# An expert's gate/up product in two halves with two signals, in place of one product with one signal

## The reference

```python
def hier_moe(x, rg_w, rg_b, re_w, re_b, w_gu, w_down):
    ...                                   # router: 2 of 32 experts for each of 512 tokens
    padded = (counts + MOE_BLOCK - 1) // MOE_BLOCK * MOE_BLOCK
    ...                                   # tokens sorted by expert, in blocks that belong to one expert each
    def expert_block(args):
        xb, e = args
        hg, hu = jnp.split(xb @ w_gu[e], 2, axis=-1)    # w_gu[e]: 1024 x 1024, gate and up
        return (jax.nn.silu(hg) * hu) @ w_down[e]       # w_down[e]: 512 x 1024
    y = lax.map(expert_block, (x_buf, block_e)).reshape(n_rows, D)
    y = y * gate_buf[:, None].astype(y.dtype)
    out = jax.ops.segment_sum(y, tok_buf, num_segments=n_tok + 1)[:n_tok]
```

## Time and profile before

| | |
|---|---|
| runs | 3419.12, 3424.94, 3429.10 us |
| profiled execution: time, span | 3429.10, 3427.3 us |
| TensorE busy, matmul / weight load | 87% / 63% of the span |
| VectorE, ScalarE, GpSimd busy | 38%, 26%, 8% |
| L1950 (gate/up), matmul | 414.7 us busy, 134.6 us idle before it |
| L1935 (gather), matmul | 204.6 us busy |
| L1960 (down), matmul | 195.3 us busy, 23.0 us idle before it |
| weight queue (q1) | 601.98 MB, 48.0% of 16 engines |

### The profile page before, as it was taken

One profiled execution on the slowest core, in us unless ns is written; L12 is line 12 of the kernel. 1 busy time (PEld: TensorE's weight loads), 2 busy tenths in 40 slices (PEclk: granted clock), 3 DMA queues, 4 the chain that ended last, 5 costly groups with the idle time before them and its releaser, 6 DMA issues. The chain is left out here.

```text
span 3427.3 us, 66223 instructions
## 1 busy us (share of the span) xinstructions
PE 2981.8 (87%) x27679; PEld 2155.2 (63%) x27679; DVE 1306.6 (38%) x2324; ACT 878.6 (26%) x1554; POOL 285.6 (8%) x361
## 2 busy tenths in 40 slices
PE   7998889999898799999987899865799898899766
PEld 5765567878773678877856576532467766566432
DVE  3254434332454443322163322211587544322112
ACT  3244432221335222122262200001443333100001
POOL 1013310000302000000000000000110530000000
PEclk9999999999999899999998899987799999999997
DMA  7423223324325233242211999998222214999996
GB/s 202 103 80 142 99 48 100 92 74 116 86 62 205 61 109 98 78 118 75 73 68 58 426 388 425 426 427 357 70 59 76 57 35 157 426 425 425 427 426 274
DMA packets 375756, 638.62 MB, mean 186 GB/s; under 512 B 90437, under 2 KB 327666, under 8 KB 339450
## 3 DMA queue, kind: packets, MB, share of 16 engines
q1 hardware_dynamic: 350025, 601.98, 48.0%
q10 hardware_dynamic: 21264, 23.88, 2.0%
q0 software_dynamic: 4256, 9.68, 0.8%
HBM read 611.06 MB, written 24.38 MB: 185 GB/s over the span
## 5 line engine op out<-in xcount | busy, mean ns | idle before, releaser
L1950 PE MATMUL moe_ps<-moe_ring,moe_scratch 128*32 128x256 f32 x6464 | 414.7, 409 | 134.6 <-DMA moe_ring<-in_moe_w_gu 117.1
L1950 PEld LDWEIGHTS moe_ps<-moe_ring,moe_scratch 128*32 128x32 f32 x6464 | 250.2, 117 | 288.8 <-issue 141.1
L2138 DVE TENSOR_TENSOR moe_scratch<-moe_scratch,moe_ps 128x128 f32<-128x128 f32 x102 | 39.5, 387 | 653.9 <-ACT moe_scratch L2008 653.9
L212 PE MATMUL ffn_in_ps<-ffn_xhi,ffn_in_whi 128*128 128x512 f32 x704 | 280.8, 399 | 9.0 <-DVE ffn_xlo L408 9.0
L213 PE MATMUL ffn_in_ps<-ffn_xlo,ffn_in_whi 128*128 128x512 f32 x704 | 280.5, 398 | 0.0
L214 PE MATMUL ffn_in_ps<-ffn_xhi,ffn_in_wlo 128*128 128x512 f32 x704 | 280.1, 398 | 0.0
L1960 PE MATMUL moe_ps<-moe_ring,moe_scratch 128*32 128x256 f32 x3232 | 195.3, 380 | 23.0 <-issue 23.0
L1935 PE MATMUL moe_ps<-xT,moe_hot 128*32 128x256 f32 x3296 | 204.6, 387 | 0.0
L1960 PEld LDWEIGHTS moe_ps<-moe_ring,moe_scratch 128*32 128x32 f32 x3232 | 121.6, 110 | 80.7 <-issue 34.6
L1935 PEld LDWEIGHTS moe_ps<-xT,moe_hot 128*32 128x32 f32 x3296 | 125.5, 113 | 60.0 <-issue 8.5
L2008 ACT ACTIVATE moe_scratch<-moe_ps 128x128 f32<-128x128 f32 x102 | 28.4, 278 | 524.0 <-PE moe_ps L1950 522.0
(11 more groups left out here) (733 smaller groups left out, 5638.1 us busy)
## 6 DMA issues: line engine op xcount, KB each, us to landing
moe_ring<-in_moe_w_gu SPq DMA_DIRECT2D x128, 2048.0 KB, 34.7
moe_ring<-in_moe_w_down SPq DMA_DIRECT2D x64, 2048.0 KB, 35.4
ffn_came<-in_ffn_w_in SPq DMA_DIRECT2D x88, 512.0 KB, 5.1
na_modw<-in_ada_w SPq DMA_DIRECT2D x6, 4096.0 KB, 13.6
rga_modw<-in_ada_w SPq DMA_DIRECT2D x16, 1024.0 KB, 6.3
expert_rows<-moe_y ACTq DMA_DIRECT2D x408, 32.0 KB, 6.7
da_in_w<-in_attn_w_qkv SPq DMA_DIRECT2D x12, 1024.0 KB, 5.2
ro_w<-in_rw_w_rkv SPq DMA_DIRECT2D x24, 512.0 KB, 3.7
```

The source lines that it names most:

```text
L212: nc.tensor.matmul(ps[0:width, slot * tiles + o], high, xhi[:, k], start=(k == 0), stop=False)
L1950: last = nc.tensor.matmul(psGU[j * BLK:(j + 1) * BLK].rearrange("p (g a n) -> p g a n", g=2, a=2), xbT[:, k], cols[:, j], start=(k == 0), ...
L2138: V.tensor_tensor(h.rearrange("p (a m i) -> p a i m", a=2, m=2), gated.rearrange("p (a i m) -> p a i m", a=2, m=2), psU.rearrange("p (a i ...
```

## The change

The gate/up product is cut by columns into two halves `a`. Each half is 64 gate and the matching 64 up columns in each of the four groups. The loop over `a` is the outer one: half 0 runs over all eight slices, then half 1 over all eight again. A half has its own PSUM bank (3 and 4 in place of bank 3 alone) and its own semaphore. SiLU, the multiply and the turn run once for each half, and the down product waits for the first half of `hT` before its slices 0 and 1 and for the second before slices 2 and 3. SyncE's release of the slots of parts 0 and 1 now goes by the second half's semaphore.

```diff
-            psG, psU, psGU, psY = ps[:, 3, 0:P], ps[:, 3, P:2 * P], ps[:, 3, 0:2 * P], ps[:, 5, 0:D // 4]
+            psGU, psY = ps[:, 3:5, 0:P], ps[:, 5, 0:D // 4]
...
-                        sp.wait_ge(down_done if part == 2 else gu_done, end)
+                        sp.wait_ge(down_done if part == 2 else gu_done[1], end)
...
-                    for k in range(KD):
-                        if k == KH:
-                            unit_here(1)
-                        cols = ring[...].rearrange("p (g a j n) -> p j g a n", g=2, a=2, j=4)
-                        for j in range(4):
-                            last = nc.tensor.matmul(psGU[j * BLK:(j + 1) * BLK].rearrange(...), xbT[:, k], cols[:, j],
-                                                    start=(k == 0), stop=(k == KD - 1))
-                    last.then_inc(gu_done, 1)
+                    for a in range(2):
+                        for k in range(KD):
+                            if a == 0 and k == KH:
+                                unit_here(1)
+                            cols = ring[...].rearrange("p (g a j n) -> p a j g n", g=2, a=2, j=4)[:, a]
+                            for j in range(4):
+                                last = nc.tensor.matmul(psGU[j * BLK:(j + 1) * BLK, a], xbT[:, k], cols[:, j], start=(k == 0), stop=(k == KD - 1))
+                        last.then_inc(gu_done[a], 1)
...
-                    pe.wait_ge(h_ready, b + 1)
                     for k in range(KH):
+                        if k % 2 == 0:
+                            pe.wait_ge(h_ready, b * 2 + k // 2 + 1)
...
-                    act.wait_ge(gu_done, b + 1)
-                    nc.scalar.activation(gated, psG, ACT.Silu).then_inc(silu_done, 1)
+                    for a in range(2):
+                        act.wait_ge(gu_done[a], b + 1)
+                        nc.scalar.activation(gated[:, a], psGU[:, a, 0:HD], ACT.Silu).then_inc(silu_done, 1)
...
-                    dve.wait_ge(silu_done, b + 1)
-                    V.tensor_tensor(h.rearrange(...), gated.rearrange(...), psU.rearrange(...), ALU.mult).then_inc(h_made, 1)
-                    dve.wait_ge(h_made, b + 1)
-                    V.transpose(hT, h).then_inc(h_ready, 1)
+                    for a in range(2):
+                        dve.wait_ge(silu_done, b * 2 + a + 1)
+                        V.tensor_tensor(h[:, a].rearrange(...), gated[:, a].rearrange(...), psGU[:, a, HD:P].rearrange(...), ALU.mult).then_inc(h_made, 1)
+                        dve.wait_ge(h_made, b * 2 + a + 1)
+                        V.transpose(hT[:, a * HD:(a + 1) * HD], h[:, a]).then_inc(h_ready, 1)
```

More of the change, by code:

```diff
@@ L1790, in norm_moe @@
             hT = scratch[:, KD * BLK:KD * BLK + P]
-            gated, h = (scratch[:, c:c + P] for c in (KD * BLK + P, KD * BLK + 2 * P))
+            gated, h = (scratch[:, c:c + P].rearrange("p (a n) -> p a n", a=2) for c in (KD * BLK + P, KD * BLK + 2 * P))
             y = sb(s2, "y", [P, 2, D // 4])
@@ L1813, in norm_moe @@
             y_stored = [B.sem(f"{N}y_stored{s}") for s in range(2)]
-            gu_done = B.sem(N + "gu_done")
+            gu_done = [B.sem(f"{N}gu_done{a}") for a in range(2)]
             all_stored = B.sem(N + "all_stored")
@@ L1944, in expert_block @@
                     unit_here(0)
-                    for k in range(KD):
-                        if k == KH:
-                            unit_here(1)
-                        cols = ring[:, (PARTS * e + k // KH) % UNITS, k % KH].rearrange("p (g a j n) -> p j g a n", g=2, a=2, j=4)
-                        for j in range(4):
-                            last = nc.tensor.matmul(psGU[j * BLK:(j + 1) * BLK].rearrange("p (g a n) -> p g a n", g=2, a=2), xbT[:, k], cols[:, j],
-                                                    start=(k == 0), stop=(k == KD - 1))
-                    last.then_inc(gu_done, 1)
+                    for a in range(2):
+                        for k in range(KD):
+                            if a == 0 and k == KH:
+                                unit_here(1)
+                            cols = ring[:, (PARTS * e + k // KH) % UNITS, k % KH].rearrange("p (g a j n) -> p a j g n", g=2, a=2, j=4)[:, a]
+                            for j in range(4):
+                                last = nc.tensor.matmul(psGU[j * BLK:(j + 1) * BLK, a], xbT[:, k], cols[:, j], start=(k == 0), stop=(k == KD - 1))
+                        last.then_inc(gu_done[a], 1)
                     pe.wait_ge(hot_ready, b + 2)
@@ L1974, in _ @@
                 pe.sem_inc(x_gathered, 1)
-                pe.sem_inc(gu_done, 1)
+                pe.sem_inc(gu_done[0], 1)
+                pe.sem_inc(gu_done[1], 1)
                 pe.sem_inc(down_done, 1)
@@ L2136, in gate_and_turn @@
                 def gate_and_turn(b, s, j):
-                    dve.wait_ge(silu_done, b + 1)
-                    V.tensor_tensor(h.rearrange("p (a m i) -> p a i m", a=2, m=2), gated.rearrange("p (a i m) -> p a i m", a=2, m=2),
-                                    psU.rearrange("p (a i m) -> p a i m", a=2, m=2), ALU.mult).then_inc(h_made, 1)
-                    dve.wait_ge(h_made, b + 1)
-                    V.transpose(hT, h).then_inc(h_ready, 1)
+                    for a in range(2):
+                        dve.wait_ge(silu_done, b * 2 + a + 1)
+                        V.tensor_tensor(h[:, a].rearrange("p (m i) -> p i m", m=2), gated[:, a].rearrange("p (i m) -> p i m", m=2),
+                                        psGU[:, a, HD:P].rearrange("p (i m) -> p i m", m=2), ALU.mult).then_inc(h_made, 1)
+                        dve.wait_ge(h_made, b * 2 + a + 1)
+                        V.transpose(hT[:, a * HD:(a + 1) * HD], h[:, a]).then_inc(h_ready, 1)
                     turn_x(b + 1)
```

## The result

The changed kernel takes 3458.79 us (median of 4 runs, 3456.77 to 3461.3), the kernel before 3424.64 us (4 runs, 3419.12 to 3429.1). The ratio is 1.0100, interval 1.0087 to 1.0112: slower by 34 us. The forecast was 3427.5 us, range 3418 to 3440, with 0.14 on slower. It was wrong. The profiled execution of the changed kernel took 3453.25 us, less than any of its four, where that of before was the slowest of its four; so the two traces differ by 24 us only, and it is these 24 us that can be placed.

What follows compares the result with a forecast made beforehand. The weight stream at some 425 GB/s was taken to bound the kernel. Terms 0.2 (seven-block expert) + 1.0 and 0.5 (layer ends) + 0.8 (code) = +2.5 us on the median 3424.9 gave 3427.5 us, range 3418 to 3440.

Steps and rivals of the forecast that it cites:

- More code: TensorE's instruction queue: 8192 added instructions, 0.34 MB more on full DMA engines, +0.8 us, between 0 and 2.
- the hole: Weight stream near 1992 us, where the seven-block expert holds its slots: 5.6 us lost before, 5.5 to 8 us forecast.
- The pairs of experts: Experts of one and three blocks by turns: 1.9 us slack for four blocks, so the stream hides under +0.5 us each.
- The code rival: Expert loops: TensorE refetches the loop's start at each jump back, 2 us a repeat, +39 us, 3464 us; chance 0.08.
- Short matmuls: Gate/up product: 128 records of 128 columns take 3.44 us, +0.04 us a block; rival at 3600 us, chance 0.05.
- The halved chain: SiLU, multiply and turn in halves: already hidden inside the gather, so no gain and cost 0.
- open chain: Before the down product: idle "issue" waits would really be for `h_ready`; faster, -1.2 us, 3424 us; chance 0.04.
- The tails: Last block of each layer: part 1 awaited after a quarter of gate/up, +1.0 us first layer, +0.5 second.
- The upper end: Whole kernel: highest terms 1.3 + 0.9 + 5.2 + 2.6 + 2 = 12 us, giving 3437 and a little scatter.
- The warning signs: Expert loops: wrong if repeats start over 0.5 us after down, holes follow three-block experts, or down beats the gather.

## Why the prediction was wrong, point by point

**The step that failed** is "*More code*". It priced the added code as bytes on full DMA engines, 0.34 MB and +0.8 us. The bytes were 0.54 MB (33 pages, 1.3 us at 425 GB/s), inside the bounds of the term and beside the point. The cost of code is the wait for a page by an engine that has run out of instructions, a term that the sum left out: 66.1 us of such stalls in the trace, and +35.8 us by the run that changes nothing but the product. A page comes at most every 6 us or so beside the stream. A first block before takes one page in 7.5 us and never waits; now it takes one and a half in 7.7 us, a page every 5.1 us. By that rate it must last 1.5 x 6 = 9 us and more; the three experts of one block took 30.4 / 3 = 10.1 us.

The 24 us between the traces are +20.7 in the loop of the first layer, +5.6 in that of the second, and -2.2 outside the loops, where the code is the same. In the first layer the first gate/up product starts 2.9 us later than before (1922.69 against 1919.84), but so does the whole stage (its first sums at 1882.00 against 1879.14), ahead of any new code, so this is not the change's doing. The first expert adds 0.9, the three of one block 7.9, the seven-block one 0.3, and its last block starts 12.0 us later (2006.16, 1994.14), 9.2 us of them made in the loop. It is this block's gate/up product that frees the ring, so the hole grew from 5.6 to 15.2 us. The pairs of experts after it were to hide anything below 0.5 us a block, at 28.9 us a pair against 30.8 of loads. They now take 30.7, 33.3, 34.1 and 33.8 us (first blocks at 2013.85, 2044.53, 2077.79, 2111.90 and 2145.72): slower than the loads, hence the small holes. Together the 19.3 us of stream. With the tail of +1.45 that is 20.8, against +20.7 measured: the layer's last block result was copied at 2406.99 after a start of 1922.69, and at 2383.40 after 1919.84. So close a match is in part luck, since the 19.3 us are an estimate from rounded rates. The second layer has nearly as many stalls (18, 31.6 us) but no expert of seven blocks, and the stream hides most of them: +5.6 us, of which 0.9 is the tail and the rest a dip of the stream to 350 GB/s from 3040 to 3060 us and smaller ones.

**The code rival** (3464 us) came out near the measured time by luck, by a mechanism that didn't occur. It let repeats pay 2 us each, and they pay nothing, as rows 3 had said: the stalls are in the first pass, which I had taken for granted. In the earlier trace rows I looked only at a stretch of repeats. The stretch just ahead of it, 1937 to 1972 us, would have shown three pages for TensorE in 35 us, and that a first block takes one; it wouldn't have shown how near that is to the limit, for no first block of before waited for one.

The Trainium skill, "Runtime: NRT & Kernel Launch", section "Instruction fetch mechanics", has crossing into a new page "mostly hidden", since the sequencer issues more slowly than pages arrive. This trace disagrees: TensorE spends a page in 128 x 26.9 ns = 3.4 us of short matmuls and gets one in 6. The same section says that a branch to outside a window of two pages stalls. The runs don't bear this out: with 512 instructions and the register work a body is longer than two pages, and in the seven-block expert its repeats follow each other at 7.1 to 7.2 us with no page moving from 1982 to 2026 us. The 128 KiB that the section gives TensorE would hold such a body; no run here comes near that bound.

**Short matmuls.** +0.04 us a block: right (6.95 us). **The halved chain.** 0: right, by its own run, and for the early start in the trace: the second turn ends at 2004.13 us, down starts behind the gather at 2004.43. So the "open chain" rival falls too. (The prediction said that the dense stretch has no idle time before down; the trace before has 2.21 us there, at 1958.07, in the first block of the seven-block expert. Nothing was built on it.) **The tails.** The last block of each layer, changed kernel:

```profile
2398.57 4.88 PE L1951 MATMUL moe_ps<-moe_ring,moe_scratch 128*32 128x128 f32 x96 [3.15 <-DMA moe_ring<-in_moe_w_gu]
2403.28 1.90 PE L1935 MATMUL moe_ps<-xT,moe_hot 128*32 128x256 f32 x32
2405.01 1.90 PE L1961 MATMUL moe_ps<-moe_ring,moe_scratch 128*32 128x256 f32 x32
```

```profile
3403.40 4.25 PE L1951 MATMUL moe_ps<-moe_ring,moe_scratch 128*32 128x128 f32 x96 [3.83 <-DMA moe_ring<-in_moe_w_gu]
3407.47 1.90 PE L1935 MATMUL moe_ps<-xT,moe_hot 128*32 128x256 f32 x32
3409.20 1.90 PE L1961 MATMUL moe_ps<-moe_ring,moe_scratch 128*32 128x256 f32 x32
```

From part 1 to down 6.44 and 5.80 us, against 4.99 and 4.90: +1.45 and +0.9, forecast +1.0 and +0.5. In the first layer the low clock lasted longer than I took: it was granted at 0.50 from 2398.57 to past 2402.00, where I had 3.3 us of it, and the 96 records took 4.88 us, not 4.2. **The upper end** of the sum had 2.6 us for the second layer's tail, where its own term said up to 5.2, with no reason given; with 5.2 it would be 3440, still far below 3459. **The warning signs** I had named were the right ones: holes did show behind experts of three blocks (in the windows at 2100 and 2140 us).

Still open: what makes up the 5 of the 6 us that are not the page's own transfer; how many pages are read ahead (after the seven-block expert the first crossings cost nothing); and 10 of the 34 us, which no trace places: they are the distance of the two profiled executions from their medians.

## What to carry to other kernels

Count the instructions of a loop body in pages of some 250, and ask how often new code is entered while transfers fill the DMA engines: there a page came every 6 us at best, and a body that used them faster stalled in its first pass, though every repeat ran clean. Halving the columns of a product doubles its instructions, so the same arithmetic may cross that line; 320 instructions a block were free here and 384 cost 1%. And splitting a chain that is already hidden behind other work gains nothing, so nothing stands against such a price.

## What the runs showed of the hardware

A TensorE program's code comes in packets of 16.4 KB on a queue that shares the 16 DMA engines with the data. In the weight stream of some 425 GB/s the closest packets were 5.8 to 6.0 us apart, beside 20 to 85 GB/s 3.3 to 4.3 us, and a packet took 0.93 us to move. An engine out of code shows only as "issue" in the middle of a run of equal instructions, 252 to 256 instructions apart; no semaphore explains it, and in the full stream it ended 2.2 to 2.5 us after a packet began to move.
